# Raw attention rows to the projection, a sliced GpSimd product in the scan, and one modulation block per layer in the retention

## The chip, the cores and the metric

The kernel runs on one NeuronCore of a Trainium2 chip. The core has TensorE (PE, matrix products into the eight banks of PSUM; PEld is its weight load), VectorE (DVE), ScalarE (ACT), GpSimd (POOL) and SyncE (SP, which here only issues DMAs). Each runs its own stream of instructions; they meet at semaphores. SBUF is the on-chip memory of 128 partitions, HBM (DRAM) the large one. The metric is the device time of one execution in microseconds; everything is float32.

## The reference

Two layers (DEPTH 2) of a diffusion backbone over 1024 latent tokens `x` and 256 context tokens `xc`, model width D = 1024. Cut to what the change touches:

```
mod = silu(c) @ w_ada[l] + b_ada[l]          # 6*D columns: sh1 sc1 ga1 sh2 sc2 ga2; once for c, once for c_ctx
z   = modulate(rms_norm(x, g_norm1[l]), sh1, sc1) @ w_in[l]
# four groups of 256 channels from z
y_conv = rms_norm(b * conv3(cg * h), g_out_conv)
y_mla  = rms_norm(softmax_attend(q, k, v), g_out_mla)      # 4 heads of 64, the norm over all 256 channels
y_rwkv = scan in two directions over the tokens, then (y + sum(r * k_sum * r_k) * v) * gate,
         k_sum = kt of the forward direction + kt of the backward one
y_ret  = silu(g) * rms_norm_per_head(retention forward + backward) * g_norm
x   = x + ga1 * (concat(y_conv, y_mla, y_rwkv, y_ret) @ w_out[l])
x   = x + ga2 * mixture_of_experts(modulate(rms_norm(x, g_norm2[l]), sh2, sc2))
rms_norm(t, g) = t * rsqrt(mean(t*t) + 1e-6) * g
```

The context tokens go through the same, except that in the last layer nothing of their output is needed.

## The kernel before

The 1280 tokens are ten tiles of 128, tiles 0 and 1 the context. The program is a chain of stages, each a block with a stream written by hand for each engine, and a stage ends for all engines together: `stage_norm1`, `stage_project_mla` (latent projection), `stage_mla_attend`, `stage_project` (all other columns of `w_in`), `stage_retention` (two blocks: states, then outputs), `stage_rwkv_prep` and `stage_rwkv_scan` twice (head pairs p = 0, 1), `stage_rwkv_out`, `stage_out` (output projection, second norm, router), `stage_topk`, `stage_moe`. All run once per layer. There is no scheduler: the order on each engine is the order of the code.

**Modulation rows.** The 6 x 1024 modulation columns of a layer are formed in blocks of 2048. A block (class `ModRows`) is eight products, one for each 128 rows of `w_ada`: a load of 1 MB on SP's queue into one of `ring` slots (`load`, L207), four matmuls of 512 columns into one PSUM bank (`product`, L216), then one addition of the bias on VectorE (`add_bias`, L224) and four stores to HBM (`store`, L230). A block (l, c0) is columns c0 to c0 + 2048 of layer l. The rows are read again from HBM by later stages. The first block of layer 0 is formed in `stage_norm1`. Two blocks, columns 2D and 4D of layer 0, are formed in the latent projection of layer 0 (`MOD_PREP`), two products per token tile; three blocks, the whole of layer 1, in the output stage of layer 0 (`MOD_OUT`), in its first nine tiles, with 3, 3, 2, 3, 3, 2, 3, 3 and 2 products; VectorE adds a block's bias in tiles 2, 5 and 8.

**Attention.** For each query tile of 128 rows there are two units, one per pair of heads: scores (L1006), softmax on VectorE and ScalarE, turns of the probabilities (L1018), the value product (`values`, L1031), the turn of its result back (`outputs`, L1039) and VectorE's division by the row sums into `o` (L1102). The loop over steps s holds a unit's scores and the turns of an earlier one; value products stand in even steps, `outputs` in odd ones. Per query tile, ScalarE squares `o` (L1141), VectorE forms the variance (L1107), GpSimd the power (L1066), VectorE scales into `on` (L1091); at steps with s % 4 == 3, `mixed` turns `on` (L1045), and ScalarE copies the two turned tiles with the gain `go` into rows 2 and 3 of `yT` (L1123). Value, output and normed tiles share PSUM bank `OB`.

**Projection.** `stage_project` runs 512-column jobs on TensorE (L526, L529); ScalarE and VectorE evacuate them in turn from a ring of six banks. Between the jobs behind `tok0` lies the convolution group: its product, its square, sums of squares by matmuls with a matrix of ones (`squares_sum`, L513) into banks 6 and 7, variance, logarithm and exponential, and the product with the gain.

**Retention, second half.** For token tile n: `scores` (L1362), decay on VectorE into `pt`, `outputs` (L1375, L1377), square and variance and power, `gated` (L1425), and `turned` (L1386) with ScalarE's scaled copy into `yT`. Two banks, `TB` = (2, 7), hold the turned tiles. On SP's queue the 13 loads of `load_rwkv_params` (L1152 to L1158) run, with a wait for all of them. Layer 0 has ten tiles here, layer 1 eight.

**Scan.** `stage_rwkv_scan` has ten steps. GpSimd forms two sets of masked tiles in each (L1968, L1975) and, behind the last step, one product of 128 x 1280 for `KS`, the sum of keys that `stage_rwkv_out` reads (L1977). VectorE scales the state by the decay (L1884, `s_Se<-s_S,rw_ET`), twice per step and direction.

## Time and profile before

| | us |
|---|---|
| median of 3 runs | 4340.51 (4336.57 to 4342.79) |
| profiled execution, own time | 4334.16 |
| its span | 4332.3 |
| TensorE busy | 3847.7 (89%) |
| VectorE, ScalarE, GpSimd busy | 1408.7, 813.0, 457.9 |
| latent projection of layer 0 | 60.6 to 181.6 |
| attention of layer 0 | 181.6 to 388.3 |
| projection of layer 0 | 388.3 to 783 |
| retention of layer 0, second half | 828 to 861.9 |
| retention of layer 1, second half | 3067.7 to 3104.4 |
| output stage of layer 0 | 1186 to 1393 |

The median is over separate executions; the profiled one is a single execution, and all other rows are from it. A busy share is an average over stages. Because a stage ends for all engines together, the time of each can be read by itself, and what one engine does in it is worth something only where it is the last. TensorE's granted clock is given as a share of full speed, 2.4 GHz; 0.50 is 1.2 GHz.

### The profile page before, as it was taken

What the parts mean: (1) busy time and instruction counts of PE and PEld (TensorE: products, weight loads), DVE (VectorE), ACT (ScalarE), POOL (GpSimd) and SP (SyncE); (2) the same over time, 40 slices, a digit from 0 to 9 for tenths busy, and PEclk for the clock granted to TensorE, in tenths of its full rate; (3) what the DMA queues carried; (4) which work ended last, traced back from release to release, by engine and by line L of the source; (5) the groups of instructions that cost most, each with busy time, mean ns of one, the idle gap of its engine ahead of it and who ended that gap; (6) DMA issues with size and microseconds to landing.
All of it is one profiled execution on the core that took longest, in us unless ns stands there. A gap on an engine that the chain in (4) does not pass through costs nothing. (4 is left out here: it accounts for less than half of the span.)

```text
span 4332.3 us, 59839 instructions
## 1 busy us (share of the span) xinstructions
PE 3847.7 (89%) x25466; PEld 2160.1 (50%) x25466; DVE 1408.7 (33%) x3018; ACT 813.0 (19%) x1840; POOL 457.9 (11%) x697
## 2 busy tenths in 40 slices
PE   6898999677897699999997898998697895999998
PEld 4555445466744344444443654444486552444444
DVE  3452112687634200000002443113777533101010
ACT  3342010344311000000002343011434210000000
POOL 1100000321200000000001100000331100000000
PEclk8999999788998899999998899999698997999999
DMA  6201110200174666666663001110100328888884
GB/s 229 107 1 30 54 54 1 74 13 18 41 281 189 246 247 246 247 250 246 245 240 116 25 4 30 56 46 26 59 4 18 109 83 308 303 322 304 321 304 158
DMA packets 190040, 612.73 MB, mean 141 GB/s; under 512 B 34472, under 2 KB 42920, under 8 KB 183120
## 3 DMA queue, kind: packets, MB, share of 16 engines
q1 hardware_dynamic: 169232, 542.30, 33.4%
q0 software_dynamic: 20544, 66.60, 5.2%
q8 instruction: 203, 3.33, 0.3%
q14 instruction: 61, 0.50, 0.0%
HBM read 561.07 MB, written 47.79 MB: 141 GB/s over the span
## 5 line engine op out<-in xcount | busy, mean ns | idle before, releaser
L2506 PE MATMUL ps<-moe_w,e_xT 128*128 128x512 f32 x1024 | 450.8, 598 | 0.8 <-ACT e_xT L2568 0.8
L2543 PE MATMUL ps<-moe_w,e_hT 128*128 128x512 f32 x1024 | 445.9, 593 | 6.1 <-ACT e_hT L2587 6.1
L2513 PE MATMUL ps<-moe_w,e_xT 128*128 128x512 f32 x1024 | 444.7, 592 | 0.0
L526 PE MATMUL ps<-hT,p_w 128*128 128x512 f32 (+1 forms) x880 | 327.1, 534 | 0.0
L2506 PEld LDWEIGHTS ps<-moe_w,e_xT 128*128 128x128 f32 x1024 | 194.9, 192 | 246.8 <-issue 245.6
L2513 PEld LDWEIGHTS ps<-moe_w,e_xT 128*128 128x128 f32 x1024 | 194.6, 190 | 244.9 <-issue 244.9
L2609 DVE TENSOR_TENSOR e_hid<-e_hid,ps 128x512 f32<-128x512 f32 x64 | 43.9, 686 | 838.1 <-PE ps L2513 838.1
L2543 PEld LDWEIGHTS ps<-moe_w,e_hT 128*128 128x128 f32 x1024 | 192.0, 190 | 239.0 <-issue 239.0
L2190 PE MATMUL ps<-M,yT 128*128 128x512 f32 x576 | 259.7, 606 | 9.8 <-DMA o_br<-in_b_router_dram 6.3
L526 PEld LDWEIGHTS ps<-hT,p_w 128*128 128x128 f32 x880 | 167.2, 190 | 159.3 <-issue 153.1
L1006 PE MATMUL ps<-M 96*128 96x512 f32 (+1 forms) x400 | 184.1, 546 | 5.9 <-ACT a_pr L1130 3.9
L2190 PEld LDWEIGHTS ps<-M,yT 128*128 128x128 f32 x576 | 108.7, 193 | 146.2 <-issue 138.1
L2619 DVE SCALAR_TENSOR_TENSOR e_ye<-ps,all_gate,e_rows 128x1024 f32<-128x1024 f32 x32 | 41.1, 1284 | 427.3 <-PE ps L2543 427.3
L2580 ACT ACTIVATE e_hid<-ps 128x512 f32<-128x512 f32 x64 | 34.7, 595 | 716.0 <-PE ps L2506 716.0
L890 PE MATMUL ps<-yT,hT 128*128 128x272 f32 (+1 forms) x608 | 146.9, 397 | 9.6 <-PEq L262 9.2
L1018 PEld LDWEIGHTS ps<-all_tabs,a_pr 128*128 128x128 f32 x656 | 74.7, 142 | 128.4 <-issue 87.5
L890 PEld LDWEIGHTS ps<-yT,hT 128*128 128x128 f32 x608 | 115.0, 196 | 41.5 <-issue 20.0
L529 PE MATMUL ps<-yT,hT 128*128 128x512 f32 (+1 forms) x320 | 131.5, 571 | 0.0
L529 PE MATMUL ps<-p_w,hT 128*128 128x512 f32 (+1 forms) x320 | 130.8, 571 | 0.0
L526 PE MATMUL ps<-hT,yT 128*128 128x512 f32 (+1 forms) x320 | 128.9, 567 | 1.9 <-PEq L990 1.9
L1018 PE MATMUL ps<-all_tabs,a_pr 128*128 128x128 f32 x656 | 111.6, 284 | 19.3 <-ACT a_pt L1075 13.8
L1096 DVE TENSOR_REDUCE a_mx<-ps 128x1 f32<-128x1280 f32 (+1 forms) x72 | 98.5, 1368 | 56.3 <-PE ps L1006 56.3
(357 smaller groups left out, 5522.4 us busy)
## 6 DMA issues: line engine op xcount, KB each, us to landing
moe_w<-in_w_gate_dram SPq DMA_DIRECT2D x64, 2048.0 KB, 12.9
moe_w<-in_w_up_dram SPq DMA_DIRECT2D x64, 2048.0 KB, 10.7
moe_w<-in_w_down_dram SPq DMA_DIRECT2D x64, 2048.0 KB, 17.0
o_mod_w<-in_w_ada_dram SPq DMA_DIRECT2D x24, 1024.0 KB, 10.3
m_mod_w<-in_w_ada_dram SPq DMA_DIRECT2D x16, 1024.0 KB, 5.9
p_w<-in_w_in_dram SPq DMA_DIRECT2D x6, 2048.0 KB, 7.9
r_z<-z_rows SPq DMA_DIRECT2D x20, 512.0 KB, 3.4
z_rows<-p_zo POOLq DMA_DIRECT2D x36, 256.0 KB, 2.3
```

The costliest lines, as they stand in the source:

```text
L526: ins = nc.tensor.matmul(ps[:, j % NB, 0:tw], w[n % RW][:, k, m * P:(m + 1) * P], hT[:, k, t0:t0 + tw], start=(k == 0), stop=(k == KT - 1))
L529: ins = nc.tensor.matmul(ps[:, j % NB, 0:hi - lo], hT[:, k, m * P:(m + 1) * P], w[n % RW][:, k, lo:hi], start=(k == 0), stop=(k == KT - 1))
L890: ins = nc.tensor.matmul(ps[:, ZBANK[a], 0:hi - lo], hT[:, k, t * P:(t + 1) * P], w[:, k, lo:hi], start=(k == 0), stop=(k == KT - 1))
L1006: ins = nc.tensor.matmul(ps[:, SB[u % 2] + i, 0:w], QT[0:QK, h, t * P:(t + 1) * P], KTr[0:QK, h, n:n + w], start=True, stop=True)
L1018: ins = nc.tensor.transpose(ps[:, TB, k * P:(k + 1) * P], pr[:, u % NP, (k0 + k) * P:(k0 + k + 1) * P], g.ident)
L1096: link(nc.vector.reduce_max(mx[:, s % 2, 0:1], src, AX_X))
L2190: ins = nc.tensor.matmul(ps[:, 2 * (n % 2) + half, :], yT[:, k, t * P:(t + 1) * P], g.M[:, k, half * 512:(half + 1) * 512], start=(i == 0) ...
L2506: ins = nc.tensor.matmul(ps[:, c, :], xT[:, 4 * half + k], wp[:, k, c * 512:(c + 1) * 512], start=(half == 0 and k == 0), stop=(half == 1 ...
L2513: ins = nc.tensor.matmul(ps[:, 2 + c, :], xT[:, 4 * half + k], wp[:, k, c * 512:(c + 1) * 512], start=(half == 0 and k == 0), stop=(half = ...
L2543: ins = nc.tensor.matmul(ps[:, 6 + c, :], hT2[:, 4 * half + k], wp[:, k, c * 512:(c + 1) * 512], start=(half == 0 and k == 0), stop=(half ...
L2609: nc.vector.tensor_tensor(hid[:, h], hid[:, h], ps[:, 2 + c], ALU.mult).then_inc(*hd.up())
L2619: nc.vector.scalar_tensor_tensor(ye[:, e % 2], bank(ps, 6, D), g.gate[:, 0, e:e + 1], rows[:], ALU.mult, ALU.mult).then_inc(*yd.up())
```

## The change

Four things change.

*Attention and projection.* The norm leaves the attention: `mixed` turns the raw `o`, at steps with s % 4 == 2 in place of 3, and ScalarE makes one plain copy into `yT`. The value product waits for that copy instead of `outputs`. In `stage_project` the norm is applied to rows 2 and 3 of `yT` for all tokens at once, in the places `M[:, 6:8]` and with sums of squares two and more jobs ahead of those of the convolution.

*Scan.* The product for `KS` is cut in ten slices of 128 columns, one behind the masks of each step.

*Modulation.* `MOD_PREP` and `MOD_OUT` lose their last block, columns 4D. A block (l, 4D) is formed in the retention's second half of each layer, with a ring of two slots that lie over the first half's buffers (`flat`), one product behind the scores of a tile, from the second tile on, and the rest behind the loop. SP issues two loads and the bias ahead of the parameter loads and the other six behind; at the end it stores the rows and waits until they have landed. In the latent projection the product of a tile is one instead of two, and in the output stage the 16 products stand at tiles 2 to 7.

*Buffers.* The products take bank 7, so the turned tiles have the one bank 2, and `turned(n)` waits for the copy of tile n - 1. `z`, `qk` and `kz` become parts of `flat`; `ra`, `rb` and `pt` share `turning`.

```diff
-MOD_PREP = [(0, 2 * D), (0, 4 * D)]
-MOD_OUT = [(1, 0), (1, 2 * D), (1, 4 * D)]
+MOD_PREP = [(0, 2 * D)]
+MOD_OUT = [(1, 0), (1, 2 * D)]
+MOD_RET = 4 * D
...
+                    if j == tok0 + MSUM_AT:
+                        pe.wait_ge(*sqd.at(1))
+                        if need_ctx:
+                            squares_sum(6, 0, 6)
+                        squares_sum(6, 1, 7)
+                    if j == tok0 + MSUM2_AT:
+                        pe.wait_ge(*vard.at(1))
+                        squares_sum(6, 2, 6)
...
+                    if j == tok0 + MSQ_AT:
+                        nc.scalar.activation(M[:, 6:8, y0:T], yT[:, 2:4, y0:T], ACT.Square).then_inc(*sqd.up())
...
+                            nc.vector.scalar_tensor_tensor(yT[:, 2 + i, y0:T], yT[:, 2 + i, y0:T], gm[:, i:i + 1], M[:, 6, y0:T],
+                                                           ALU.mult, ALU.mult)
...
-                        mod.product(pe, 2 * j - 4)
-                        mod.product(pe, 2 * j - 3)
+                        mod.product(pe, j - 2)
...
-                    if k >= 4:
-                        pe.wait_ge(*ye.at((k - 2) // 2))
+                    if k >= 3:
+                        pe.wait_ge(*ye.at((k - 1) // 2))
...
-                        if i == 1 and s >= 11 and s % 4 == 3:
-                            mixed((s - 11) // 4)
+                        if i == 1 and s >= 10 and s % 4 == 2:
+                            mixed((s - 10) // 4)
...
-                        for i in range(2):
-                            ins = nc.scalar.activation(yT[:, 2 + i, t * P:(t + 1) * P], ps[:, OB, (2 + i) * P:(3 + i) * P],
-                                                       ACT.Copy, scale=go[:, i:i + 1])
-                        ins.then_inc(*ye.up())
+                        nc.scalar.copy(yT[:, 2:4, t * P:(t + 1) * P], ps[:, OB, 2 * P:4 * P].rearrange("p (a n) -> p a n", a=2)).then_inc(*ye.up())
...
+                mod.load(sp, 0)
+                mod.load(sp, 1)
+                mod.load_bias(sp)
                 load_rwkv_params(sp, g, I, l, R_rwkv, small)
+                for j in range(2, MOD_LOADS):
+                    mod.load(sp, j)
+                mod.store(sp, 0)
+                sp.wait_ge(*mod.stored.at(64))
...
+                    if 1 <= n <= MOD_LOADS:
+                        mod.product(pe, n - 1)
+                for j in range(N - 1, MOD_LOADS):
+                    mod.product(pe, j)
                 turned(N - 2)
                 turned(N - 1)
...
+                mod.add_bias(dve, 0)
...
-                nc.gpsimd.tensor_tensor(R["KS"][p][:], R["KS"][p][:], M[:, p], ALU.mult)
+                    ts = slice(s * P, (s + 1) * P)
+                    nc.gpsimd.tensor_tensor(R["KS"][p][:, ts], R["KS"][p][:, ts], M[:, p, ts], ALU.mult)
...
-            b, i = divmod(n, 3)
-            return range(MOD_LOADS * b + 3 * i, MOD_LOADS * b + min(3 * i + 3, MOD_LOADS)) if b < len(MOD_OUT) else range(0)
+            b, i = divmod(n - 2, 3)
+            return range(MOD_LOADS * b + 3 * i, MOD_LOADS * b + min(3 * i + 3, MOD_LOADS)) if 0 <= b < len(MOD_OUT) else range(0)
...
-                    if mod and n < N and n % 3 == 2:
-                        mod.add_bias(dve, n // 3)
+                    if mod and n in (4, 7):
+                        mod.add_bias(dve, (n - 2) // 3)
```

What stands in a row on TensorE in two steps of the attention of layer 0, before: score matmuls (`M`), turns of probabilities (`a_pr`), value product (`mla_V`), turn of the normed tile (`a_on`) and of the value product's result (`a_ot`).

```order
L1031 MATMUL ps<-a_pt,mla_V 64x128 x20
L1006 MATMUL ps<-M 128x512
L1018 MATMUL ps<-all_tabs,a_pr 128x128 x4
L1006 MATMUL ps<-M 128x512
L1018 MATMUL ps<-all_tabs,a_pr 128x128 x4
L1045 MATMUL ps<-all_tabs,a_on 128x128 x2
L1006 MATMUL ps<-M 128x256
L1018 MATMUL ps<-all_tabs,a_pr 128x128 x2
L1039 MATMUL ps<-all_tabs,a_ot 128x128
```

And after, in the same place:

```order
L1033 MATMUL ps<-all_tabs,a_pr 128x128 x4
L1058 MATMUL ps<-all_tabs,a_o 128x128 x2
L1021 MATMUL ps<-M 128x256
L1033 MATMUL ps<-all_tabs,a_pr 128x128 x2
L1046 MATMUL ps<-a_pt,mla_V 64x128 x20
L1021 MATMUL ps<-M 128x512
L1033 MATMUL ps<-all_tabs,a_pr 128x128 x4
L1021 MATMUL ps<-M 128x512
L1033 MATMUL ps<-all_tabs,a_pr 128x128 x4
L1021 MATMUL ps<-M 128x256
L1033 MATMUL ps<-all_tabs,a_pr 128x128 x2
L1052 MATMUL ps<-all_tabs,a_ot 128x128
```

The turn of the tile now stands in the even step, ahead of the value product and not ahead of the turn of its result.

TensorE in the retention's second half, before: scores (`r_QT`), outputs (`r_SF`, `r_SB`, `r_V`) and the turn of a gated tile (`r_on`).

```order
L1362 MATMUL ps<-r_QT 128x128 x4
L1386 MATMUL ps<-all_tabs,r_on 128x128 x2
L1375 MATMUL ps<-r_SF,r_QX 128x128
L1375 MATMUL ps<-r_SB,r_QX 128x128
L1377 MATMUL ps<-r_V,r_pt 128x64 x2
```

And after:

```order
L1360 MATMUL ps<-r_QT 128x128 x4
L1384 MATMUL ps<-all_tabs,r_on 128x128 x2
L217 MATMUL ps<-r_flat,all_cond 32x512 x4
L1373 MATMUL ps<-r_SF,r_QX 128x128
L1373 MATMUL ps<-r_SB,r_QX 128x128
L1375 MATMUL ps<-r_V,r_turning 128x64 x2
```

A product (L217) stands between the turn and the next tile's outputs.

SP's queue in the same stage, after (before, only the 13 parameter loads stand there):

```order
L1145 DMA rw_rk<-in_rwkv_r_k_dram 128x2x1
L1145 DMA rw_gln<-in_g_ln_x_dram 128x2x1
L1146 DMA rw_g<-in_rwkv_g_dram 128x256
L208 DMA r_flat<-in_w_ada_dram 128x2048 x6
L231 DMA mod_rows<-r_mod_b 2x512 x4
```

The six later loads and the stores follow the parameter loads on the one queue.

## Rows read from the trace of the kernel before

**Rows 1.** Stretches in windows, retention's second half: start:end, length, busy PE PEld DVE ACT POOL, PEclk...

```profile
828.00:861.90 33.90, 30.18 (x260) 27.27 (x260) 21.18 (x62) 9.85 (x30) 22.93 (x29) 0.90 0.08 13
3067.70:3088.00 20.30, 18.92 (x100) 17.66 (x101) 8.10 (x22) 1.78 (x5) 14.33 (x20) 0.50 0.12 21
```

**Rows 2.** Waits of TensorE, attention of layer 0 (181 to 388 us): total us, times, longest

```profile
PE ps L1039 <- ACT yT L1123: 9.5, 9, 1.1
```

**Rows 3.** Timeline of TensorE, same attention: start us, length us, instruction, [idle before]

```profile
263.93 1.12 PE L1006 MATMUL ps<-M 96*128 96x512 f32 x2
...
268.06 1.02 PE L1006 MATMUL ps<-M 96*128 96x512 f32 x2
...
274.40 1.13 PE L1006 MATMUL ps<-M 96*128 96x512 f32 x2
...
279.80 1.02 PE L1006 MATMUL ps<-M 96*128 96x512 f32 x2
```

**Rows 4.** Timeline of VectorE and TensorE, end of the same attention

```profile
384.60 0.29 DVE L1102 TENSOR_TENSOR a_o<-ps,a_rc 128x128 f32<-128x128 f32 x1
...
386.69 0.69 PE L1045 MATMUL ps<-all_tabs,a_on 128*128 128x128 f32 x2 [2.33 <-DVE a_on L1091]
```

**Rows 5.** Timeline of TensorE, projection of layer 0, a sum of squares

```profile
598.79 1.88 PE L513 MATMUL ps<-M,all_tabs 128*128 128x512 f32 x4
```

**Rows 6.** Timeline of PE, DVE and SP: modulation products, output stage's ninth tile

```profile
97.67 1.92 PE L216 MATMUL ps<-m_mod_w,all_cond 128*32 128x512 f32 x16
...
1373.24 1.04 PE L2200 MATMUL ps<-all_tabs,o_h 128*128 128x128 f32 x8
...
1376.31 0.69 DVE L224 TENSOR_TENSOR o_mod_b<-ps,o_mod_b 128x512 f32<-128x512 f32 x1 [8.37 <-PE ps L216]
1376.92 1.22 DVE L2245 TENSOR_TENSOR o_xo<-ps,o_rows 128x1024 f32<-128x1024 f32 x1
...
1377.03 1.11 SPq L230 DMA_DIRECT2D mod_rows<-o_mod_b  x4
```

**Rows 7.** Timeline of GpSimd, end of layer 0's second scan

```profile
1140.88 1.28 POOL L1975 TENSOR_TENSOR s_NL<-s_UM,rw_nlev 128x128 f32<-128x128 f32 x3 [0.33 <-DVE s_UM L1912]
1142.12 2.88 POOL L1977 TENSOR_TENSOR rw_KS<-rw_KS,M 128x1280 f32<-128x1280 f32 x1
```

**Rows 8.** Timeline of VectorE, the same stretch

```profile
1129.98 0.65 DVE L1884 TENSOR_SCALAR s_Se<-s_S,rw_ET 128x64 f32<-128x64 f32 x2
...
1137.90 0.65 DVE L1884 TENSOR_SCALAR s_Se<-s_S,rw_ET 128x64 f32<-128x64 f32 x2
...
1142.31 2.74 DVE L1884 TENSOR_SCALAR s_Se<-s_S,rw_ET 128x64 f32<-128x64 f32 x1
...
1149.26 0.53 DVE L1884 TENSOR_SCALAR s_Se<-s_S,rw_ET 128x64 f32<-128x64 f32 x2
```

**Rows 9.** Timeline of TensorE, retention's second half, layer 0

```profile
844.26 0.44 PE L1386 MATMUL ps<-all_tabs,r_on 128*128 128x128 f32 x2
...
847.01 0.44 PE L1386 MATMUL ps<-all_tabs,r_on 128*128 128x128 f32 x2
...
860.34 0.69 PE L1386 MATMUL ps<-all_tabs,r_on 128*128 128x128 f32 x2 [2.10 <-DVE r_on L1425]
```

**Rows 10.** Timeline of SyncE's queue, parameter loads of that stage

```profile
827.90 0.38 SPq L1152 DMA_DIRECT2D rw_w<-in_rwkv_w_dram  x1
...
835.45 0.47 SPq L1158 DMA_DIRECT2D rw_g<-in_rwkv_g_dram  x1
```

**Rows 11.** Landing times of the latent projection's modulation weights

```profile
DMA to landing us min/median/max: 4.8/5.9/10.0
```

**Rows 12.** Page, section 6, stores of 256 KB: KB each, us to landing

```profile
z_rows<-p_zo POOLq DMA_DIRECT2D x36, 256.0 KB, 2.3
```

**Rows 13.** Stretches in windows, behind layer 0's second scan's GpSimd product

```profile
1144.00:1146.00 2.00, 0.34 (x10) 0.37 (x12) 1.90 (x4) 0.00 (x0) 1.01 (x1) 1.00 0.00 0
1146.00:1148.00 2.00, 2.00 (x52) 2.00 (x49) 0.98 (x5) 0.53 (x2) 0.00 (x0) 0.52 0.03 8
```

More of the change, by code:

```diff
@@ L572, in conv @@
                             dve.wait_ge(*ev[1].at(tok0 // 2))
-                            dve.wait_ge(*small.at(80))
+                            dve.wait_ge(*small.at(96))
                             if not need_ctx:
@@ L587, in conv, with variance @@
                         nc.vector.tensor_tensor(y, y, M[:, i], ALU.mult).then_inc(*prod.up())
-                def variance(spans, b):
+                def variance(r, spans, n):
                     for s in spans:
                         t0, tw = SPANS[s]
-                        dve.wait_ge(*csum.at(s + 1))
-                        ins = nc.vector.tensor_scalar(M[:, 0, t0:t0 + tw], ps[:, 6 + s % 2, 0:tw], 1.0 / GW, EPS, ALU.mult, ALU.add)
+                        dve.wait_ge(*csum.at(n + s))
+                        ins = nc.vector.tensor_scalar(M[:, r, t0:t0 + tw], ps[:, 6 + s % 2, 0:tw], 1.0 / GW, EPS, ALU.mult, ALU.add)
                     ins.then_inc(*vard.up())
@@ L992, in _ @@
             def _(sp):
-                with nc.allow_non_contiguous_dma(reason="vectors into columns"):
-                    sp.dma_start(go[:], col(I["g_out_mla"][l], 2)).then_inc(*small.up(16))
                 sp.dma_start(first_weights(g), I["w_in"][l].rearrange("(k p) f -> p k f", p=P)[:, :, 0:512]).then_inc(*pw_in.up(16))
@@ L1060, in _ @@
                         outputs((s - 5) // 2)
-            @block.gpsimd
-            def _(pool):
-                for n in range(NQ):
-                    pool.wait_ge(*g.vr.at(n + 1))
-                    nc.gpsimd.tensor_tensor(ss[:, 1:2], ss[:, 1:2], g.mhalf[:, 0:1], ALU.pow).then_inc(*g.rq.up())
             def turned_copy(eng, copy, u, i, done):
@@ L1104, in _ @@
                                                 rc[:].unsqueeze(2).broadcast_to([P, 2, HD]), ALU.mult).then_inc(*od.up())
-                    if s >= 9 and s % 4 == 1 and (s - 9) // 4 < NQ:
-                        dve.wait_ge(*sqd.at((s - 9) // 4 + 1))
-                        nc.vector.tensor_scalar(ss[:, 1:2], ss[:, 0:1], 1.0 / GW, EPS, ALU.mult, ALU.add).then_inc(*g.vr.up())
             @block.scalar
             def _(act):
-                act.wait_ge(*small.at(16))
                 for s in range(NU + 8):
@@ L1246, in rotated @@
                                                          r[:, 1, a:a + 32].unsqueeze(1).broadcast_to([P, 8, 32]), ALU.mult))
-                        nc.vector.tensor_tensor(q, ra[:], rb[:], ALU.add).then_inc(*qkd.up())
+                        nc.vector.tensor_tensor(q, ra, rb, ALU.add).then_inc(*qkd.up())
                 def scaled_queries(t):
```

108 lines of the change are left out of this document (51 added, 57 removed).

## The prediction

> **What bounds the kernel now.** The page comes first: TensorE is busy for 89% of the span and sets the end of nearly every stage, so an edit is worth what it takes from or adds to TensorE's stream, or to the few places where TensorE stands still. Then the windows by stage, and in them the waits and the timeline. The second half of the retention is TensorE's too: busy 30.18 of 33.90 us in layer 0 [rows 1]. The attention is TensorE's with one repeating gap: the turn of the attention output waits for ScalarE's scaled copy, 9.5 us in 9 waits in layer 0 [rows 2]. In the scan VectorE and TensorE alternate, and the view to read is VectorE's timeline beside GpSimd's. The mixture of experts is not touched.
>
> **The sum** is made against the profiled execution, 4334.16 us (span 4332.3). The median of the three runs is 4340.51, 6.35 above; I carry the difference over unchanged.
>
> **1. Attention: the gap goes.** Per query tile the norm (square, variance, power, scaling) leaves ScalarE, VectorE and GpSimd, and the turn of the tile moves one step earlier. An odd step without it runs from 263.93 to 268.06, 4.13 us; the odd step with it from 274.40 to 279.80, 5.40 us, in which the wait of about 1.1 lies [rows 2, 3]. Two things make the 1.27: the wait, and the order in which a turn and a copy follow. In the new even step the two transposes lie where TensorE waits for ScalarE's copy of a score tile anyway, so they cost nothing there. The wait is not simply deleted: the value product now waits for the raw copy. That copy is issued right behind the score-tile copy, while TensorE does two more transposes, so I expect 0.1 us; the bounds are 0 and the whole 1.1. In steady state 8 tiles of layer 0 and 6 of layer 1 have it: 14 x (1.27 - 0.1) = -16.4. At each end, from the last output (384.60) to its turn (386.69) 2.09 us pass, of which the output itself is 0.29 and a hand-over 0.1 [rows 4]; 1.7 goes, and one copy instead of two saves 0.3. -4.0 for two layers. Together **-20.4**, bounds -7 and -22.
>
> **2. Projection: the norm comes back in large.** The sums of squares are now matmuls of ones with 1280 columns twice (1024 twice in layer 1). A pair of 512-column matmuls reads 1.88 us [rows 5], of which some 0.15 overlaps its neighbours: 2.5 x 1.73 + 2 x 1.73 = **+7.8**. All of it is on the path, since TensorE never pauses there. The rest is covered: ScalarE's square of 2560 elements and its second logarithm and exponential, and VectorE's variance and two more scaled products, stand in engines with free time between their evacuations of the ring of six banks. That cover ends only if they take more than about 10 us in a row; I put the longest, four scaled products and an evacuation, near 7. Without it each us over costs one. The extra load of the gain vector on SP's queue is issued long before its use.
>
> **3. Modulation products that leave.** Two products read 1.92 us [rows 6], so one is 0.95, a little more with the change of weights. Eight leave the latent projection of layer 0, one per tile, where TensorE doesn't wait: 8 x 1.0 = **-8.0**. Eight leave the output stage, those of its first two tiles and of its ninth. Six cost 0.95 each. The two of the ninth tile also hold VectorE, which adds the bias only at 1376.31 and starts on the last tile at 1376.92, though its matmuls had ended by 1373.24 [rows 6]: 3.5 of that goes. **-9.2**. What is late next in this tail is the same chain of norm and softmax that layer 1 has.
>
> **4. KS product in slices.** One GpSimd product of 128x1280 stands behind the last masks of each scan (2.88 us from 1142.12). VectorE's small scaling, two of which take 0.53 us at 1149.26, starts at 1142.31 and lasts 2.74, to just past GpSimd's end, and everything behind it is late: the step lasts 11.36 us (1137.90 to 1149.26) against 7.92 before it (from 1129.98) [rows 7, 8]. Four scans have this. The bounds for one are 2.48 (VectorE's alone) and 3.44 (the whole step, TensorE having fallen to half clock behind the gap); I take 3.0, so -12. A slice of 128x128 should last like the mask product of that size, 1.28 us for three. It stands behind them in every step, and starts about 0.2 us before the same small scaling. Where two such scalings meet mask products today (at 1137.90) they take 0.65 instead of 0.53 [rows 7, 8], 0.06 more for each; half of it on the path in 36 steps is +1. **-11**, bounds -6 and -13.
>
> **5. One product block per layer in the retention's second half.** It is what the change pays. *Products:* layer 0 has eight among its ten tiles, all ahead of the last output, in a stream without gaps (one tile is 2.75 us, 844.26 to 847.01): 8 x 1.0 = 8.0. In layer 1 the granted clock is 0.50, level 1.2 GHz, for the stage's first 20 us, until 3088 [rows 1]. Two products fall there at 1.95, four behind at 1.0: 7.9. The last two fit partly into the 2.10 us for which TensorE waits for the last tile anyway (as at 860.34) [rows 9]. *Loads:* the ring has two slots. The third load is queued on SP behind the 13 parameter loads, whose last one is issued 7.55 us after the first [rows 10], and behind the wait for their landing, taken as 2.3 us. With two weight and four bias issues in front it goes out near 13 us after the start and lands 4.8 to 5.9 us later [rows 11], at 18 to 19. The third product is reached at 16: 2 us of wait in layer 0, none in layer 1, whose stream is slower. After that a slot is refilled when its product ends and wanted again 2 x 2.75 + 0.95 = 6.4 us later, which 4.8 to 5.9 meets. In layer 1 the eighth product follows the seventh at once and waits some 2 us. *Clock:* in the scan TensorE fell from 1.00 to 0.52 behind a stretch in which it was busy 0.34 of 2 us [rows 13]; for the wait in layer 0 I add 1.5. *End:* the stage now closes with the bias (0.69 us), a hand-over (0.4), four stores (1.11 us to issue [rows 6]) and their landing; before, nothing but a turn and a scaled copy stood there, 1.5 us from 860.34 to 861.9. No row shows the landing of such a store; the 256 KB stores of the page need 2.3 [rows 12], so 2.2. 4.4 less 1.5 is +2.9 in layer 0; in layer 1, with the late eighth product, +4.2. Sum: 8.0 + 2.0 + 1.5 + 2.9 = 14.4, and 7.9 + 4.2 = 12.1; **+26.5**, bounds +17 and +38.
>
> The Trainium skill, page "DMA: Bandwidth & Descriptors", section "Anatomy of one DMA — SWDGE (gpsimd) path", prices a transfer's fixed part at about 2.0 us and calls a write to HBM the heaviest case. By it the end would cost an estimated 0.2 us less or somewhat more than above; no run here shows it.
>
> **Result:** -20.4 + 7.8 - 8.0 - 9.2 - 11 + 26.5 = -14.3 us. 4319.9 for a profiled execution, **4326 us** for the median.
>
> **Rivals.**
> *Loads starve the retention (slower).* Nothing says that a slot is refilled in time: the slowest load of the latent projection took 10.0 us [rows 11]. Then product j+2 comes 0.3 + 10.0 + 1.0 = 11.3 us after product j instead of 7.4: 3.9 more per pair, some three pairs a layer, +23, and a few us at half clock, +2. Net +11, **4351 us**. It decides from 2.4 us per pair, a landing of 8.5 us. Against it: the 10.0 belongs to three loads in flight behind small ones; the median is 5.9. Chance 0.09. The Trainium skill says in "TensorE: Matmul & The Clock Gate", section "HAM oscillation — how this bites in real kernels", that waits for loads between groups of matmuls send TensorE to its half clock each time. Had that come with every wait, this rival would be worse by the same again; rows 13 show the fall once.
> *The attention's wait only changes places.* If ScalarE reaches the raw copy a full copy late, the value product waits 0.9 and edit 1 is worth 14 x 0.3 + 4 = 8: **4338 us**, within 0.2%. For it speaks that ScalarE has three jobs in that step; against, that it stands idle before each. Chance 0.10.
> *The slices hold VectorE in each step.* If each of 40 slices costs 0.2 us on the chain, edit 4 is worth -4: **4333 us**. Chance 0.11. The Trainium skill ("GPSIMD Engine Reference", section "1. Specifications") has GpSimd contend with VectorE's two-port modes and with instructions of two SBUF inputs. The products behind the small scaling read one input from PSUM, so by that rule they aren't held; rows 8 agree as far as they go: what is held beside GpSimd is the scaling, from SBUF to SBUF.
> *TensorE's clock comes up sooner in layer 1.* The products are long matmuls in a stretch that stood at 1.2 GHz until 3088. Some 3 to 5 us less: **4322 us**. Chance 0.08.
>
> **How the numbers follow.** Forecast 0.62, rivals as above. A measurement of this kernel can tell about 0.2%, 8.7 us, so faster begins below 4331.8. Of the forecast's 0.62 nearly all is there, with the sooner clock and half of the slices' case: 0.71. Same: the attention's case, the other half of the slices', the forecast's edge: 0.21. Slower: the starved loads, 0.08. The range comes from the bounds of edits 1, 4 and 5, which do not all fall one way: 14 below and above the forecast, 4312 to 4340.
>
> **What would show it.** Right: in the attention the turn of the output without a wait, and step pairs of about 10.4 us; the small scaling never over 0.5 us; the output stage without VectorE's wait at the ninth tile; the retention's second half at some 48 us in layer 0. Wrong: value products that wait more than 0.3 us for ScalarE; loads in the retention that land after 8 us; a half-clock stretch of more than 4 us in its second half in layer 0; TensorE waiting in the projection behind the new sums.

## The result and the profile after

| | before | changed |
|---|---|---|
| median of 3 runs, us | 4340.51 | 4311.6 (4306.37 to 4313.94) |
| ratio to before | | 0.9932, interval 0.991 to 0.9955 |
| profiled execution, own time | 4334.16 | 4311.6 |
| its span | 4332.3 | 4309.8 |

The change made the kernel 28.9 us faster in the median. The forecast was 14.3 us faster, 4326, with a range of 4312 to 4340: the direction was right, the size was about half of what came, and the time lies 0.4 us below the range. A later comparison with more runs, told below, gives 25.8 us less between medians and a ratio of 0.9948 (0.9933 to 0.9964), with the kernel before at 4334.5.

The two profiled executions by stage, each from its first TensorE instruction to that of the next stage:

| stage | before | changed | difference | forecast |
|---|---|---|---|---|
| latent projection, layer 0 | 121.0 | 115.1 | -5.9 | -8.0 |
| attention, layers 0 and 1 | 206.7, 191.3 | 192.6, 180.6 | -14.1, -10.7 | -20.4 together |
| projection | 398.9, 351.4 | 401.6, 353.4 | +2.8, +1.9 | +7.8 together |
| retention, second half | 34.1, 36.7 | 45.5, 44.2 | +11.4, +7.4 | +14.4, +12.1 |
| output stage, layer 0 | 244.9 | 235.6 | -9.3 | -9.2 |
| four scans | 353.9 | 341.3 | -12.6 | -11 |
| four rwkv preparation stages | 234.3 | 242.2 | +7.8 | 0 |
| all the rest | | | -1.3 | 0 |

The stages that the change touches give -29.0 us, the preparation stages, whose code is the same, take 7.8 back.

**Attention.** Waits of TensorE in the attention of layer 0 of the changed kernel (total us, times, longest). It answers to [rows 2]; the turn of the output is L1052 now.

```profile
PE ps L1033 <- ACT a_pt L1082: 6.7, 24, 0.7
...
PE ps L1052 <- ACT a_ot L1129: 0.8, 3, 0.4
PE ps L1046 <- ACT yT L1119: 0.6, 1, 0.6
```

The wait of 9.5 us is gone, and the value product, which now carries the wait for the raw copy, waits once, 0.6 us, at the end. Two steps of TensorE's timeline there, from one value product to the next, answer to [rows 3]:

```profile
250.18 2.40 PE L1046 MATMUL ps<-a_pt,mla_V 128*64 128x128 f32 x40
252.52 1.12 PE L1021 MATMUL ps<-M 96*128 96x512 f32 x2
...
256.53 0.27 PE L1052 MATMUL ps<-all_tabs,a_ot 128*128 128x128 f32 x1
...
259.44 0.38 PE L1058 MATMUL ps<-all_tabs,a_o 128*128 128x128 f32 x2
...
260.65 2.40 PE L1046 MATMUL ps<-a_pt,mla_V 128*64 128x128 f32 x40
```

260.65 less 250.18 is 10.47 us for a pair of steps; before, the pair with the turned norm took 11.75 and the other 10.47. The turn (L1058) fits in without a wait.

**Projection.** One of the sums that came in, and the windows of the stage's first microseconds (start:end, length, busy PE PEld DVE ACT POOL, granted clock, DMA share, GB/s), changed kernel:

```profile
506.03 2.74 PE L517 MATMUL ps<-M,all_tabs 128*128 128x256 f32 x8
```

```profile
368.50:372.00 3.50, 3.50 (x16) 3.12 (x17) 2.20 (x1) 0.00 (x0) 0.00 (x0) 1.00 0.65 184
```

The same window of the kernel before:

```profile
388.30:391.70 3.40, 3.35 (x8) 2.75 (x9) 2.20 (x1) 0.00 (x0) 0.00 (x0) 0.50 0.64 188
```

The sums cost what [rows 5] said: this one, a pair of 256 columns and a pair of 512, holds the stream for 2.58 us (506.03 to 508.61), the three others 1.72 each, 7.7 in all. But the stage began at the half clock, 0.50, before, and at 1.00 now.

**Output stage and modulation.** In the latent projection a product by itself, against 1.92 for two [rows 6], and in the output stage VectorE's work on the tile that followed the last product before:

```profile
97.10 1.06 PE L217 MATMUL ps<-m_mod_w,all_cond 128*32 128x512 f32 x8
```

```profile
1360.51 1.23 DVE L2249 TENSOR_TENSOR o_xo<-ps,o_rows 128x1024 f32<-128x1024 f32 x1 [5.50 <-PE ps L2194]
1361.77 1.22 DVE L2250 TENSOR_TENSOR o_xo<-o_xo,o_xi 128x1024 f32<-128x1024 f32 x1
```

VectorE no longer waits for a product there (PE L2194 is the tile's own matmul): the step that [rows 6] showed is gone as forecast.

**Scan.** GpSimd at the end of layer 0's second scan, then VectorE's small scaling over the whole kernel (duration in ns, least, median, most):

```profile
1136.82 0.45 POOL L1978 TENSOR_TENSOR s_NL<-s_UM,rw_nlev 128x128 f32<-128x128 f32 x1 [1.00 <-DVE s_UM L1915]
1137.60 1.28 POOL L1978 TENSOR_TENSOR s_NL<-s_UM,rw_nlev 128x128 f32<-128x128 f32 x3 [0.33 <-DVE s_UM L1915]
1138.84 0.46 POOL L1981 TENSOR_TENSOR rw_KS<-rw_KS,M 128x128 f32<-128x128 f32 x1
```

```profile
L1887 DVE TENSOR_SCALAR s_Se<-s_S,rw_ET x160: 248/317/473, 923.4 to 3374.6; 128x64 f32<-128x64 f32 x160
```

A slice takes 0.46 us behind three masks, and the longest of 160 small scalings is 0.47 us, where [rows 8] had one of 2.74. Their median is 0.32 us and was 0.26 (0.255) before.

**Retention, second half.** TensorE in layer 0 (the answer to [rows 9]): turn, product, the next tile's outputs, then the same one tile later; and the one wait for a load.

```profile
828.60 1.06 PE L217 MATMUL ps<-r_flat,all_cond 128*32 128x512 f32 x8 [1.22 <-DMA r_flat<-in_w_ada_dram]
...
840.05 0.44 PE L1384 MATMUL ps<-all_tabs,r_on 128*128 128x128 f32 x2
840.41 1.07 PE L217 MATMUL ps<-r_flat,all_cond 128*32 128x512 f32 x8
841.41 0.49 PE L1373 MATMUL ps<-r_SF,r_QX 128*128 128x128 f32 x2
...
844.35 1.06 PE L217 MATMUL ps<-r_flat,all_cond 128*32 128x512 f32 x8
```

A tile takes 3.94 us (840.41 to 844.35) against 2.75, so a product costs 1.19. The third product waits 1.22 us. The stage's end, on VectorE and on SyncE's queue, and the next stage's first instruction:

```profile
853.49 0.68 DVE L225 TENSOR_TENSOR r_mod_b<-ps,r_mod_b 128x512 f32<-128x512 f32 x1
```

```profile
823.67 18.20 SPq L208 DMA_DIRECT2D r_flat<-in_w_ada_dram  x6
854.20 1.14 SPq L231 DMA_DIRECT2D mod_rows<-r_mod_b  x4
856.73 0.36 SPq L1529 DMA_DIRECT2D rp_wide<-const_reset_dram  x1
```

```profile
853.63 0.69 PE L1384 MATMUL ps<-all_tabs,r_on 128*128 128x128 f32 x2 [1.65 <-DVE r_on L1427]
856.77 2.04 PE L1544 MATMUL ps<-M,rw_wa 64*128 64x256 f32 x4 [2.45 <-PEq L1339]
```

The bias ends at 854.17, the stores are issued by 855.34, and 1.4 us later the next stage starts: 3.1 us behind the last turn, where it was 1.6 (860.34 to 861.9) [rows 1, 9]. The stage itself began with 4.1 us at 0.50 (811.3 to 815.4), as before the change.

### The profile page after: what moved, and what is told of

Read it like the earlier page. It is cut to its first block and busy times, and to the rows that moved or that the text cites. A ratio compares the mean times of both kernels' runs of the same rounds, so it can differ in the third digit from the quotient of the medians.

```text
span 4309.8 us, 59771 instructions
## 1 busy us (share of the span) xinstructions
PE 3851.3 (89%) x25486; PEld 2158.0 (50%) x25486; DVE 1402.8 (33%) x2991; ACT 809.3 (19%) x1792; POOL 453.6 (11%) x715
## 5 line engine op out<-in xcount | busy, mean ns | idle before, releaser
L2194 PE MATMUL ps<-M,yT 128*128 128x512 f32 x576 | 258.0, 603 | 10.9 <-DMA o_br<-in_b_router_dram 7.1
L2194 PEld LDWEIGHTS ps<-M,yT 128*128 128x128 f32 x576 | 108.2, 192 | 144.6 <-issue 135.7
## 6 DMA issues: line engine op xcount, KB each, us to landing
o_mod_w<-in_w_ada_dram SPq DMA_DIRECT2D x16, 1024.0 KB, 10.2
```

The costliest lines, as they stand in the source:

```text
L2194: ins = nc.tensor.matmul(ps[:, 2 * (n % 2) + half, :], yT[:, k, t * P:(t + 1) * P], g.M[:, k, half * 512:(half + 1) * 512], start=(i == 0) ...
```

## The experiments

Twelve runs were made; `whole`, `before2`, `order2` and `tuned2` repeat a kernel. Ratios are to the kernel before on the same chip, and the us behind a ratio are that ratio times its time.

**The parts apart.** `attn` is the kernel before with the functions of the attention and the projection alone, `slices` with that of the scan, `mods` with the blocks of modulation (latent projection, retention, output stage), and `whole` the changed kernel again.

> The kernel before with the attention and projection part alone. Theory A (the parts add up, and the trace of the changed kernel shows each at its size): attention -14.1 and -10.7 us, projection +2.8 and +1.9, together -20 us against the kernel before. Forecast's terms: -20.4 + 7.8 = -12.6. Rival B (the projection's small cost comes from where the throttle fell in that one execution, not from the change): attention -25, projection up to +7.8, together -17. In all of them the rwkv preparation stages keep 58 to 60 us.

> The kernel before with the sliced KS product alone. Theory A: each of the four scans ends 3 us earlier (no small scaling over 0.5 us, last step 7.9 instead of 11.3 us), -12 to -12.5 us. Forecast's term: -11. Rival: the preparation or output stage behind a scan gets longer by 2 to 3 us because TensorE's granted clock falls elsewhere, so that only -6 is left.

> The kernel before with the modulation blocks moved alone. Theory A (terms of the trace add): latent projection -5.9, output stage -9.3, retention +11.4 and +7.4: +3.6 us. Rival C (the longer preparation stages seen in the changed kernel, +3.7 and +3.4, belong to the moved blocks): +11 us, with preparation stages of 62 us. Forecast's terms: -8.0 - 9.2 + 26.5 = +9.3.

> The changed kernel once more, for a second profile of it. Theory A (terms add, the longer preparation stages were chance of the throttle): -28 us in the median. Rival C (they belong to the change): -22.5 us in the median, and the same preparation stages at 62 us in this profile.

| run | median, us | ratio, interval | forecast's terms |
|---|---|---|---|
| before | 4334.47 (20 runs) | 1 | |
| attn | 4316.34 | 0.9961 (0.9948 to 0.9974), -17 | -12.6 |
| slices | 4322.14 | 0.9975 (0.9965 to 0.9985), -11 | -11 |
| mods | 4345.4 | 1.0024 (1.0012 to 1.0035), +10 | +9.3 |
| whole | 4308.72 | 0.9948 (0.9933 to 0.9964), -23 | -14.3 |

The three parts give -17, -11 and +10, -18 together, against -23 for all, inside the intervals. The slices are worth what was forecast; in their profile the four scans took 341.4 us instead of 353.9. The attention with its projection gives 4 us more than its terms, though -12.6 is still inside its interval. Its profile has -11.7 and -10.7 for the attentions, +2.8 and +0.4 for the projections, -19.2 in all, so the small price of the projection repeats and rival B's up to +7.8 doesn't come. The moved blocks, by themselves, cost what was forecast, and not the +3.6 that the stages of the changed kernel's trace add up to (their interval is +5 to +15). The second profile of the changed kernel has attentions of 192.5 and 180.6 us, projections of +2.7 and +1.95, retentions of 45.6 and 44.3: these repeat. Its preparation stages are 60.0, 60.2, 60.0 and 58.4: those don't. The time of `whole`, 23 us less by the ratio and 26 by the medians, lies between theory A's 28 and rival C's 22.5 and doesn't tell them apart.

In its profile, what `mods` pays more than the changed kernel for the moved blocks lies in one place: its retention of layer 0 took 50.3 us, while its latent projection (-5.2), its output stage (-11.5) and its retention of layer 1 (+7.5) cost no more. TensorE at its third product, and the windows of the stage:

```profile
839.45 0.44 PE L1396 MATMUL ps<-all_tabs,r_on 128*128 128x128 f32 x2
843.10 1.93 PE L217 MATMUL ps<-r_flat,all_cond 128*32 128x512 f32 x8 [3.21 <-DMA r_flat<-in_w_ada_dram]
```

```profile
825.20:842.00 16.80, 14.26 (x132) 11.26 (x132) 9.95 (x28) 2.78 (x8) 13.55 (x19) 1.00 0.74 222
842.00:852.30 10.30, 9.20 (x43) 5.20 (x43) 2.20 (x6) 1.01 (x3) 2.97 (x4) 0.50 0.58 215
852.30:875.50 23.20, 18.00 (x151) 12.76 (x151) 9.89 (x29) 6.11 (x20) 6.49 (x8) 0.94 0.42 136
```

The stage started at clock 1.00, came to the third product sooner, and waited 3.2 us for the same load. The clock fell at 842.0, 2.1 us into the wait, and 10.3 us at 0.50 followed, products of 1.93 us among them. In the changed kernel a wait of 1.2 us at the same product was followed by no fall (granted clock 1.00 from 815.4 to 852.9). The forecast's +14.4 for this stage, with its 2.0 and 1.5 for wait and clock, lies between the two outcomes, 11.4 and 16.2. That the time of `mods` meets the forecast's +9.3 is therefore partly luck: it holds a stretch at half clock that the changed kernel had in neither of its profiles.

**Is it the wait?** `order` and `mods_order` are the changed kernel and `mods` with SyncE's wait for the parameters behind the six loads.

```diff
     sp.dma_start(R["g2"][:], I["rwkv_g2"][l]).then_inc(*done.up(16))
-    sp.wait_ge(*done.at(16 * RWKV_LOADS))
...
                 for j in range(2, MOD_LOADS):
                     mod.load(sp, j)
+                sp.wait_ge(*small.at(16 * RWKV_LOADS))
                 mod.store(sp, 0)
```

> The changed kernel with SyncE's wait for the 13 parameter loads moved behind the six later weight loads (the parameter loads keep their place). Theory E (the third product waits for a load that this wait delays by about 2 us): the third product of layer 0 without its wait of 1.2 to 1.4 us, retention's second half 44.2 us instead of 45.5; layer 1 unchanged at 44.3, since the last product's wait of 1.9 hangs on the ring; -1.4 us. Rival (the 13 parameter loads themselves delay it): wait of 1 us or more left, no change.

> The modulation move alone, with SyncE's wait moved in the same way. Theory F (in the modulation move alone TensorE's 10 us at half clock in the retention of layer 0 follow from the 3.2 us wait for the third load): wait 1 us or less, no such stretch, stage 45 us instead of 50.3; -5 us against that kernel. Rival G (the stretch comes from where the stage lies, not from the wait): stage 47 to 48, the stretch still there.

> The same kernel as in the run order, for a second profile. Theory L (TensorE's 15 us at half clock at the start of the retention of layer 0 in that run were not due to the moved wait): stage 44.2 us, half clock for about 4 us. Rival (they were): 49.5 us again.

| run | ratio | retention, layer 0 | wait for the load | half clock in the stage |
|---|---|---|---|---|
| whole | 0.9948 | 45.6 | 1.4 | 8.0 |
| order | 0.9940 | 49.5 | none | 18.8 |
| order2 (one execution) | | 44.7 | 0.6 | 7.1 |
| mods | 1.0024 | 50.3 | 3.2 | 12.9 |
| mods_order | 1.0027 | 46.4 | 1.9 | 5.5 |

The third load shows what the move did. It went out 12.4 us behind the stage's start in `whole` and 12.9 in `mods`, and at 11.2 in `order2` and `mods_order`: SyncE's wait for the parameters had held it back for 1.2 to 1.7 us. The waits of TensorE shrank to 0.6 and 1.9 us, where theory E had none and theory F 1 us or less; what is left stands behind the 13 parameter loads themselves, and with all weight loads ahead of them (`tuned`, below) the third goes out at 6.1. The missing wait of `order` shows nothing: TensorE was at half clock, its first product ended only at 13.5, and the third load, which needs that product's slot, went out at 13.6. What the stage took is another matter. The same kernel, `order`, gave 49.5 and 44.7 us; the windows at its start, first and second profile:

```profile
816.40:831.80 15.40, 15.40 (x81) 12.76 (x82) 5.89 (x16) 0.77 (x2) 9.13 (x13) 0.50 0.70 191
```

```profile
820.40:824.00 3.60, 3.56 (x23) 3.30 (x24) 1.51 (x4) 0.00 (x0) 3.20 (x6) 0.50 0.74 239
```

In the first the stage began with 15.4 us at 0.50, in the second with 3.6. So the clock at the stage's beginning, which one execution has and the next has not, moves it by 4.8 us, more than the load's wait. That the length of the fall in the middle of `mods` follows from the wait (theory F) is not shown: with the wait at 1.9 instead of 3.2 us it was 3.4 us long instead of 10.3, but in `gain` (below) the same product waited 2.2 us and no fall followed (granted clock 1.00 from 817.9 to 858.8). It is one profile of each, and the whole kernel's time shows no gain (1.0024 and 1.0027, where theory F had 5 us).

**Whose are the preparation stages' 7.8 us?** `before2` is the kernel before again, `shift` the kernel before with longer turns at the retention's end:

```diff
-                    for i in range(2):
+                    for i in range(8 if n == N - 1 else 2):
+                        i = i % 2
                         ins = nc.tensor.transpose(ps[:, TB[n % 2], i * P:(i + 1) * P], on[:, n % 2, i * P:(i + 1) * P], g.ident)
```

> The kernel before, unchanged, for a second profile of it. Theory I: its four preparation stages are not all 58.2 us again where an earlier stage came out otherwise; attention 206.7 and 191.3, retention's second half 34.1 and 36.7 within 3 us. Rival K (stages repeat to 0.3 us from one execution to the next, and only the code moves them): all the same.

> The kernel before with six transposes more on TensorE ahead of the last turn of each layer's retention (they write the same tile again; 1.6 us each time, 3.2 in all). Theory I (a preparation stage takes 58.2 to 61.9 us by where the granted clock falls in it, which goes with when it starts; the code of it has no part in it): the preparation stage behind, 58.2 us in the kernel before, takes 59.5 to 61.6 in at least one of the two layers, and the whole is longer by 3 to 10 us. Rival J (the longer preparation in the changed kernel belongs to its stores and its buffers in the retention): 58.2 in both layers, +3.2 us in all.

The four preparation stages of the second profile of the kernel before:

```profile
868.50:926.90 58.40, 36.12 (x480) 27.13 (x480) 47.96 (x90) 33.56 (x45) 2.90 (x1) 0.73 0.12 38
1015.50:1073.80 58.30, 35.99 (x484) 27.07 (x485) 47.96 (x90) 33.49 (x45) 2.95 (x2) 0.73 0.09 30
3109.80:3171.50 61.70, 39.91 (x484) 29.11 (x485) 48.29 (x90) 33.67 (x45) 2.95 (x2) 0.68 0.11 36
3260.40:3322.20 61.80, 40.09 (x484) 28.91 (x485) 48.08 (x90) 33.69 (x45) 2.93 (x2) 0.65 0.09 29
```

And of `shift`:

```profile
863.90:923.30 59.40, 36.77 (x484) 27.65 (x485) 48.28 (x90) 33.65 (x45) 2.94 (x2) 0.71 0.11 37
1013.20:1074.00 60.80, 36.87 (x480) 27.48 (x481) 47.97 (x90) 33.51 (x45) 2.89 (x1) 0.71 0.09 29
3116.20:3174.10 57.90, 35.80 (x480) 26.98 (x481) 47.96 (x90) 33.54 (x45) 2.90 (x1) 0.73 0.12 38
3261.80:3323.40 61.60, 39.78 (x484) 28.68 (x485) 47.96 (x90) 33.63 (x45) 2.96 (x2) 0.68 0.09 29
```

The unchanged kernel has 58.4, 58.3, 61.7 and 61.8 us, with a granted clock of 0.73, 0.73, 0.68 and 0.65; in its first profile three of the four were 58.2. Nothing of the changed kernel is needed for a long one. Rival K, that stages repeat from one execution to the next, falls too: the attention of layer 1 took 195.7 us here against 191.3, and the execution as a whole 10.5 us more than the first. `shift` cost 0.21% (0.12 to 0.31), 9 us for the 3.2 of its transposes, which rival J's +3.2 doesn't reach; the stage behind them came out at 59.4 in layer 0, just under what theory I named, and at 57.9 in layer 1. So the 7.8 us need nothing of the change, though no run shows where they came from in that one execution. Over all fourteen profiles the four stages together took 234.3 to 244.3 us; the first profile of the kernel before is the lowest of them, and the three profiles without any of the change have 234.3, 239.7 and 240.1. The parts of a sum read from a single trace carry such amounts: 3.4 us for a preparation stage, 4.4 for an attention.

**The start of the attention.** The stage gained at its start too, which no term of the forecast had. VectorE's first row maximum and ScalarE there, kernel before, then ScalarE's first line in layer 1:

```profile
183.35 0.15 DVE L1097 TENSOR_SCALAR a_mx<-a_mx 128x1 f32<-128x1 f32 x1
183.59 1.28 ACT L1130 ACT_TABLE_LOAD   x1 [2.23 <-DVE a_mx L1097]
185.13 0.47 ACT L1130 ACTIVATE a_pr<-ps,a_mx 128x256 f32<-128x256 f32 x1 [0.26 <-DMA a_go<-in_g_out_mla_dram]
...
2490.99 1.28 ACT L1130 ACT_TABLE_LOAD   x1 [6.71 <-DVE a_mx L1097]
```

And changed, layer 0:

```profile
175.92 1.28 ACT L1124 ACT_TABLE_LOAD   x1 [0.27 <-PEq L728]
177.83 0.47 ACT L1124 ACTIVATE a_pr<-ps,a_mx 128x256 f32<-128x256 f32 x1 [0.63 <-DVE a_mx L1098]
```

Before, the table load (1.28 us), which stands ahead of the first exponential, started 1.9 us behind the stage's start (181.7), just when VectorE's first row maximum was done (183.50); in layer 1 it started 6.4 us behind (2484.6), and there too the profile names the row maximum as what released it. Changed, the table load is the first thing that ScalarE does, beside the first scores, and the row maximum is waited for behind it. ScalarE had two waits ahead of its first exponential before, one for the landing of the gain vector and one for the row maximum; it now has the second alone. The landing itself held it for only 0.26 us in layer 0 (185.13) and for nothing in layer 1. `gain` puts the load and the wait back, without any use of the vector:

```diff
+                with nc.allow_non_contiguous_dma(reason="vectors into columns"):
+                    sp.dma_start(go[:], col(I["g_out_mla"][l], 2)).then_inc(*small.up(16))
...
             def _(act):
+                act.wait_ge(*small.at(16))
```

> The changed kernel with the attention's load of the gain vector put back, and ScalarE's wait for it at the start of the stage; the vector isn't used there. Theory D (the attention starts sooner because ScalarE no longer waits for this landing ahead of its table load): attention of layer 0 194.1 us instead of 192.5, of layer 1 183.5 instead of 180.6, +4.5 us in all. Rival (the sooner start is due to something else, such as the granted clock): 192.5 and 180.6, no change.

```profile
179.74 1.28 ACT L1128 ACT_TABLE_LOAD   x1 [2.23 <-DVE a_mx L1101]
181.04 0.47 ACT L1128 ACTIVATE a_pr<-ps,a_mx 128x256 f32<-128x256 f32 x1
```

The table load is late again, again behind the row maximum, and the exponential follows it at once: nobody waits for the landing. So what costs is that there is a second wait, which leaves the table load behind the row maximum, and not how long the vector takes. How the two waits come to stand that way around the table load no row shows. From the stage's start to the first value product it took 8.94 us before, 7.36 in `whole` and 8.69 here; in layer 1, 23.21, 20.32 and 23.21. That is 1.33 + 2.89 = 4.2 us for one wait on a vector of 256 numbers. The whole stages took 193.5 and 185.8 us, where theory D had 194.1 and 183.5; in layer 1 the stage also ended at half clock, 2.2 us more behind the last value product. The kernel as a whole: 4319.33, ratio 0.9960 (0.9946 to 0.9974), against 0.9948 and 0.9932 for the changed one; the intervals overlap, so it is the stage's start that shows the loss and not the time. Theory D stands in that the sooner start comes from the wait that went, and the rival's "no change" falls; its reason, the landing, doesn't stand.

**What of the retention's price is due?** `tuned` changes that stage alone:

```diff
-    sp.wait_ge(*done.at(16 * RWKV_LOADS))
...
-                load_rwkv_params(sp, g, I, l, R_rwkv, small)
                 for j in range(2, MOD_LOADS):
                     mod.load(sp, j)
+                load_rwkv_params(sp, g, I, l, R_rwkv, small)
+                sp.wait_ge(*small.at(16 * RWKV_LOADS))
...
-                    if 1 <= n <= MOD_LOADS:
-                        mod.product(pe, n - 1)
-                for j in range(N - 1, MOD_LOADS):
-                    mod.product(pe, j)
+                    if n < MOD_LOADS:
+                        mod.product(pe, n)
...
-                    gated(n)
-                mod.add_bias(dve, 0)
+                    if n == N - 1:
+                        mod.add_bias(dve, 0)
+                    gated(n)
```

> The changed kernel with, in the retention's second half: all eight weight loads ahead of the parameter loads, the wait for these behind them, one product per tile from the first tile on, and the bias added ahead of the last tile's gating. Theory H (of the stage's extra time only the products' 9.5 us are due, the rest is the load wait and the end): layer 0 45.5 to 43 us, layer 1 44.3 to 41 us, -6 us against the changed kernel. Rival (the first product waits for its load, which lands 5 us after the start): layer 0 unchanged or up to 2 us longer.

> The same kernel as in the run tuned, timed once more against the kernel before, with another profile. Theory H: retention's second half 42.5 and 41.2 us again, ratio to the kernel before 0.993 to 0.994, 2 to 5 us better than the changed kernel. Rival (the 6 us of the stage are lost again to the granted clock behind it): ratio 0.995 as the changed kernel.

```profile
815.60:858.10 42.50, 37.34 (x325) 27.01 (x325) 21.86 (x63) 9.94 (x31) 22.91 (x29) 0.98 0.65 215
3040.70:3081.90 41.20, 35.24 (x273) 24.72 (x273) 17.96 (x51) 7.90 (x25) 20.72 (x27) 0.87 0.68 221
```

```profile
PE ps L217 <- DMA r_flat<-in_w_ada_dram: 0.7, 1, 0.7
```

The stage takes 42.5 and 41.2 us, in the second profile 43.0 and 41.3: 3 us less in each layer, as expected, and the wait is that of the first product for its load (820.52). The time is 4307.15, ratio 0.9938 (0.9924 to 0.9952), and again 4308.78, 0.9937 (0.9924 to 0.9951). The changed kernel has 0.9948 and 0.9932. So the stage was some 3 us shorter in both layers of both profiles, and the kernel perhaps by 2 us, not by theory H's 6; it can't be told from the changed kernel by these runs.

## Why the prediction was wrong in size, point by point

The step that failed is the first term of the sum, the attention: -20.4 with bounds of -7 and -22, measured -24.8, outside its own bounds. It had put the start of the stage at nothing, and the start gave 4.5 us. The second is the projection's "all of it is on the path", +7.8 where +4.7 came.

**1. Attention (-20.4, came -24.8).** The gap went as described: the raw copy costs the value product nothing in steady state, and the pair of steps lost 1.28 us where 1.17 was taken. I counted 14 tiles; 11 have the long pair, and one shorter pair (10.43) lost 1.7 us. From the first value product of a stage to the third from last 9.2 and 6.4 us went, 15.6 for the forecast's 16.4. What failed is that the removed load with its wait was costed at nothing. The time to the first value product fell by 1.6 and 2.9 us, 4.5, of which `gain` shows 4.2 to hang on that wait. The last part is the end: from the third value product from last to the next stage 27.4 us before and 24.1 after in layer 0, 25.6 and 24.1 in layer 1, 4.8 us for the forecast's 4.0. Behind the last value product alone it is 8.35 before and 4.83 after, 8.10 and 4.83 (3.52 + 3.27 = 6.8), but in layer 1 the last value product itself comes 1.8 us later against the third from last, since it is now behind the raw copy. A part of the gain is the clock, since the end of the attention lay at 0.50 before (3.4 us of it in layer 0) and not in the changed kernel; `attn`, whose end in layer 0 lay at half clock, has 6.98 there.

**2. Projection (+7.8, came +4.7).** The sums cost 7.7 us, as forecast. The stall at the end of the attention had left the projection 3.4 us at half clock in layer 0 and 6.2 in layer 1; now 0 and 3.4, and half of the difference, 3.1 us, is given back: an estimate, since a product of 1.06 us takes 1.93 at 0.50. In layer 0 this is a pattern over the profiles: in all six with the old attention the projection starts with 3.4 to 4.9 us at 0.50, and of the eight with the new one a single one does (`order2`, 5.0). In layer 1 it is 2.9 to 6.2 us in all six, and of the eight only the changed kernel's first profile and `whole` have any, 3.4 and 3.3. The step that failed is "all of it is on the path" as the whole story: a stall also costs what TensorE is slow for behind it, in the next stage.

**3. Modulation products that leave (-8.0 and -9.2, came -5.9 and -9.3).** The second product of a tile was worth 0.86 us (1.92 less 1.06), not 1.0. That is 1.1 of the 2.1 us of the latent projection. The other 1.0 is not chance: over the fourteen profiles that stage took 121.0 to 121.8 us with two products a tile and 115.0 to 115.8 with one. Why a product is worth only 0.7 there stays open.

**4. Slices (-11, came -12.6 in the profile, -11 by itself).** Right, in mechanism and size. No small scaling is over 0.5 us. The small scalings did get 0.06 us longer each, as taken from [rows 8] (median 0.255 to 0.317 us); whether that costs the +1 on the path these runs don't tell. The Trainium skill, in "GPSIMD Engine Reference", section "1. Specifications", names as what contends with GpSimd the two-port modes of VectorE and its instructions with two SBUF inputs; the scaling from SBUF to SBUF was the one held, and by a slice of 0.46 us it can't be held for 2.7.

**5. Retention (+26.5, came +18.9 in the changed kernel, +23.7 in `mods`).** The product was under-sized, 1.19 us instead of 1.0, so 9.5 instead of 8.0 in layer 0. The wait was 1.2 to 1.4 instead of 2.0, the clock's 1.5 did not come, the end cost 1.5 instead of 2.9. In layer 1 the clock rose 15.5 us into the stage instead of 20.5, as in the rival to which I gave 0.08, and saved about 2.5 us. That the products did it is not shown: with no product in the stage the clock rose after 20.5 and 20.7 us in two profiles and after 15.7 to 16.5 in the three others (`slices`, `shift`, `before2`), with the products from the second tile on after 13.9 to 16.7, and with them from the first tile on (`tuned`, `tuned2`) after 10.1 and 10.2. The last product waited 1.85 us for its load, as forecast. So in layer 0 the products were taken 1.5 us too low, and the wait, the clock and the end too high. What is left of the 7.6 us by which the term missed is in part the throttle: alone, in `mods`, the moved blocks cost +10 us, forecast +9.3.

On the two rules that were weighed: the Trainium skill, "TensorE: Matmul & The Clock Gate", section "HAM oscillation — how this bites in real kernels", tells of a kernel whose waits for loads between groups of matmuls, about 3 to 5 us each, brought TensorE to its half clock each time. Here the clock fell in the wait of 3.2 us, which agrees; the waits of 0.6 to 1.4 us and the one of 2.2 us in `gain` were shorter and brought no fall, and the one of 1.9 us in `mods_order` was followed by 3.4 us at 0.50. A fall with every wait, as it was weighed under the first rival, did not come. For the stores, the Trainium skill, "DMA: Bandwidth & Descriptors", section "Anatomy of one DMA — SWDGE (gpsimd) path", would have a fixed part of about 2.0 us for a transfer on GpSimd's path, and these stores are SyncE's; from the last store's issue (855.34) to the next stage's first instruction 1.4 us pass, and the row decides.

**The base.** I carried the 6.35 us between the profiled execution and the median over unchanged. Later medians of the kernel before are 4334.5, 4335.0 and 4336.8 with 20, 12 and 15 runs. So the profiled execution, 4334.16, was an ordinary one, and the median of three that the result is measured against lay some 5 us high. Some 4 to 6 of the 14.4 us by which the forecast missed are this, and against the later medians the change is worth about 25.

**The range.** It was built from bounds of single terms as if nothing else moved. Two causes outside of them, the unseen head of ScalarE's stream (4.5) and the clock behind a stall that goes (3.1), made up 7.6 us. The retention's term, inside its bounds, gave another 7.6 and the base 4 to 6, and the preparation stages took 7.8 back. That the time came out 0.4 us below the range and not well below it is the luck of that last draw.

None of the rivals that end higher came: no load of the block took over 8 us (4.8 to 7.7), the raw copy isn't waited for in steady state, and no scaling is held for the length of a long product. Of the signs of being wrong two showed, weakly: one value product, the last, waited 0.6 us for ScalarE, and the retention of layer 0 began with 4.1 us at half clock, which it had before the change too. The step pairs (10.47) came as said, the retention of layer 0 at 45.5 us instead of some 48.

## What to carry to other kernels

Before an instruction that waits is removed, look at the first rows of its engine in the stage: here a second wait ahead of the first exponential left a table load of 1.28 us behind the first, and that was part of the price. A stall that goes can give back, besides its own length, the half-clock time behind it, which may lie in the next stage. And a sum read from one trace should carry the spread of unchanged stages from a second one; here unchanged stages of 58 us moved by 3.4 us, as much as most terms.

## What the runs showed of the hardware

The granted clock can fall at other places in another execution of the same program, and a stage's time goes with it: preparation stages of one and the same code took 56.1 to 62.3 us over fourteen profiles; those over 61.4 in the rows above had a granted clock of 0.65 to 0.68, those of 57.9 to 58.4 us 0.73. TensorE's clock fell in a wait of 3.2 us in the middle of a busy stage, and 10.3 us at 1.2 GHz followed; a wait of 1.9 us at the same product was followed by 3.4 us, waits of 1.2, 1.4 and 2.2 us by none. A table load of 1.28 us on ScalarE started 1.9 and 6.4 us into a stage where two waits stood ahead of the first exponential, and at its start where one did. A product of modulation rows by itself takes 1.06 us, and 1.19 us of the stream between other matmuls.
